# S5 parameters prepared on GpSimd beside the first layer's projections, kept in DRAM, and S5 inputs turned beside the retention heads

## What is computed

```python
    lam = lax.complex(lam_re.astype(f32), lam_im.astype(f32))
    delta = jnp.exp(log_step.astype(f32))[:, None]
    lam_bar = jnp.exp(lam * delta)
    b_bar = ((lam_bar - 1.0) / lam)[:, :, None] * b_mat
    bu = jnp.einsum('gpc,bsgc->bsgp', b_bar, uf.astype(jnp.complex64))
    a = jnp.broadcast_to(lam_bar, bu.shape)
    _, states = lax.associative_scan(combine, (a, bu), axis=1)
    y = jnp.einsum('gcp,bsgp->bsgc', c_mat, states).real + d_skip.astype(f32) * uf
```

## Time and profile before

| | us |
|---|---|
| median of 3 runs | 3587.89 (3587.1 to 3588.26) |
| profiled execution | 3577.61 |
| its span (first to last instruction) | 3575.8 |
| mean granted clock of TensorE | 0.923 of full speed |
| busy: PE, DVE, ACT, POOL | 3150.0, 2233.1, 1674.9, 79.6 |

### The profile page before, as it was taken

One profiled execution on the slowest core, in us unless ns is written; L12 is line 12 of the kernel. 1 busy time (PEld: TensorE's weight loads), 2 busy tenths in 40 slices (PEclk: granted clock), 3 DMA queues, 4 the chain that ended last, 5 costly groups with the idle time before them and its releaser, 6 DMA issues.

```text
span 3575.8 us, 37657 instructions
## 1 busy us (share of the span) xinstructions
PE 3150.0 (88%) x14074; PEld 2471.9 (69%) x14074; DVE 2233.1 (62%) x2597; ACT 1674.9 (47%) x1936; POOL 79.6 (2%) x88
## 2 busy tenths in 40 slices
PE   5896775999999999999959747999998987899998
PEld 2652464777777777777747635788887765688887
DVE  2314444999999999999965666443445545544445
ACT  2212132878787877878753112432335234432234
POOL 0000000000000000000030000000000000000000
PEclk8897775999999999999979876999999988999999
DMA  8142123999999999999952201223232210123320
GB/s 325 53 144 92 60 64 119 368 369 375 368 375 376 372 373 371 372 369 372 365 187 67 72 0 48 68 91 101 94 107 76 83 37 1 41 87 97 97 74 24
DMA packets 226419, 637.83 MB, mean 178 GB/s; under 512 B 21225, under 2 KB 39927, under 8 KB 226135
## 3 DMA queue, kind: packets, MB, share of 16 engines
q1 hardware_dynamic: 206880, 575.35, 44.8%
q0 software_dynamic: 10512, 37.80, 2.8%
q10 hardware_dynamic: 8838, 22.23, 1.7%
HBM read 605.94 MB, written 29.36 MB: 178 GB/s over the span
## 4 chain that ended last, share of the span: by engine, by line
PE 77%; DVE 14%; ACT 5%; issue 2%; DMA 1%; POOL 0%; DVEq 0%; ACTq 0%; POOLq 0%; SPq 0%
PE ps L267 74%; ACT arena L232 3%; PE ps L279 3%; DVE arena L187 2%; DVE arena L198 2%; ACT wunits L449 2%; DVE arena L206 2%; DVE arena L194 1%; DVE ring_r L457 1%; DVE arena L210 1%; DVE ring L187 1%; DVE arena L192 1%; DVE arena_r L457 1%; DVE arena_r L198 1%; ACT arena_r L232 1%
## 5 line engine op out<-in xcount | busy, mean ns | idle before, releaser
L457 DVE TENSOR_TENSOR ring_r<-ring,wunits 128x1024 fp32r<-128x1024 f32 x795 | 943.4, 1216 | 676.9 <-ACT wunits L449 659.6
L449 ACT ACTIVATE wunits<-ring 128x1024 fp32r<-128x1024 f32 x795 | 830.6, 1054 | 824.6 <-PE ps L267 796.4
L267 PE MATMUL ps<-arena_r,wunits 128*128 128x512 f32 x3552 | 1107.5, 394 | 60.9 <-DVE ring_r L457 34.1
L267 PE MATMUL ps<-wunits,arena_r 128*128 128x512 f32 x3520 | 989.5, 398 | 3.2 <-DVE arena_r L187 3.2
L267 PEld LDWEIGHTS ps<-arena_r,wunits 128*128 128x128 f32 x3552 | 670.2, 190 | 209.1 <-DVE ring_r L457 34.2
L267 PEld LDWEIGHTS ps<-wunits,arena_r 128*128 128x128 f32 x3520 | 658.2, 189 | 148.1 <-DVE arena_r L187 5.0
L267 PE MATMUL ps<-arena_r,ring_r 128*128 128x512 f32 x1776 | 693.6, 391 | 0.0
L267 PE MATMUL ps<-ring_r,arena_r 128*128 128x512 f32 x1280 | 409.8, 390 | 0.0
L267 PE MATMUL ps<-arena 128*128 128x128 f32 (+11 forms) x1378 | 276.2, 386 | 147.9 <-DVE arena L192 32.8
L267 PEld LDWEIGHTS ps<-arena_r,ring_r 128*128 128x128 f32 x1776 | 336.6, 190 | 70.5
L267 PEld LDWEIGHTS ps<-arena 128*128 128x128 f32 (+4 forms) x1378 | 204.8, 232 | 206.1 <-issue 42.9
(11 more groups left out here) (119 smaller groups left out, 1771.3 us busy)
## 6 DMA issues: line engine op xcount, KB each, us to landing
ring<-in_w_gu SPq DMA_DIRECT2D x382, 512.0 KB, 6.7
ring<-in_w_down SPq DMA_DIRECT2D x170, 512.0 KB, 5.4
arena<-in_w_gu SPq DMA_DIRECT2D x146, 512.0 KB, 6.8
arena<-in_w_down SPq DMA_DIRECT2D x94, 512.0 KB, 5.6
ring<-in_w_ada SPq DMA_DIRECT2D x48, 512.0 KB, 4.7
ring<-in_ffn_w_gate SPq DMA_DIRECT2D x44, 512.0 KB, 3.5
ring<-in_ffn_w_up SPq DMA_DIRECT2D x44, 512.0 KB, 3.6
ring<-in_ffn_w_down SPq DMA_DIRECT2D x40, 512.0 KB, 3.6
```

The source lines that it names most:

```text
L267: ins = self.e.matmul(o, l_, r_, start=start, stop=stop, skip_group_check=True)
L449: q.inc(q.e.activation(h, raw, ACT.Copy), (st.tag, "hi", i))
L457: q.inc(q.e.tensor_tensor(lo, raw, h.bitcast(F32), ALU.subtract), (st.tag, "lo", i))
```

## The change

`s5_prep_*` is split. The 32-column part (`s5_small_*`, the old code without the 128x512 operations) is the first `slow` work of `proj`, where four steps are added (9 of its 16 steps are used). The 128x512 operations go to GpSimd (`s5_pool`), in slots 9 to 17 of the ring, which the weights of the first layer do without until "s5 parked". The PE, DVE and ACT parts of it (`s5_large_*`) come after the eight `ada` generators in `slow`; `pool` gets four steps. The tables are written to DRAM: `s5_kk`, `s5_mg` in pieces by ACT's queue, `s5_gs`, `s5_ww` by POOL's. ACT loads the first two before the projections of `ret`, POOL the others in the S5 stage. The turning of `U3` is `slow` work of `heads`. The tables of the retention are loaded before the projections, no more behind the barrier "ret in". `AB` has a buffer for each direction, cleared once by DVE. The zeros are written later, for 14 blocks and not 15. POOL is no longer waited for at barriers.

```diff
...
     def barrier_of(q, key):
-        for table, s_ in ((at_pe, s_pe), (at_dve, s_dve), (at_act, s_act), (at_pool, s_pool)):
+        for table, s_ in ((at_pe, s_pe), (at_dve, s_dve), (at_act, s_act)):
...
+            elif w.before[0] == "pool":
+                s.wait_ge(*pool(w.before[1]))
...
-    W = main_stream("w", SLOTS)
+    PARK = SLOTS[9:]
+    W = main_stream("w", SLOTS[0:9])
...
     def widen():
-        if len(W.pieces) == N_FIRST + NRING:
-            W.slots = list(reversed(MORE)) + W.slots
+        if len(W.pieces) == N_FIRST + 9:
+            for x in PARK:
+                x[3] = ("pool", "s5 parked")
+            W.slots = PARK + MORE + W.slots
...
-    def zero_pool(g):
-        g.inc(g.e.memset(ZB, 0.0), "zeros")
-        g.own()
-        load(g, "zero", y_d[4096:NBLK * 128, :].rearrange("(b p) d -> p b d", p=128),
-             ZB.unsqueeze(1).to_broadcast([128, NBLK - 32, 1024]))
...
             p.note(("w", "used", u.i))
+            p.step()
...
             p.note(("pool", g))
+            p.step()
...
+    def power(g, dst, X, XI_, i, sign, key):
+        g.tt(ptmp, XI_, bc(sl(AI, i)), ALU.mult)
+        g.tt(dst, X, bc(sl(AR, i)), ALU.mult)
+        g.tt(dst, dst, ptmp, ALU.add if sign > 0 else ALU.subtract, key)
+    def s5_pool(g):
+        g.wait_ge(*loaded("s5b"))
+        g.ts(BI[0:64, :, :], BI[0:64, :, :], -1.0, None, ALU.mult, None)
+        g.wait_ge(*dve("s5 f"))
+        g.tt(ptmp, BI, bc(FI), ALU.mult)
+        g.tt(PA, B0, bc(FR), ALU.mult)
+        g.tt(PA, PA, ptmp, ALU.add, "s5 pa")
+        g.tt(ptmp, B0, bc(FI), ALU.mult)
+        g.tt(PI_, BI, bc(FR), ALU.mult)
+        g.tt(PI_, PI_, ptmp, ALU.subtract)
+        g.wait_ge(*act("s5 qi"))
+        for tau in range(1, 9):
+            power(g, GP[:, :, tau - 1, :], QA, QI, tau, -1, ("s5 q", tau))
+        g.own()
+        g.e.dma_start(gs_d, BUF).then_inc(s_gsd, 16)
+        g.wait_ge(s_gsd, 16)
+        g.wait_ge(*pe("s5 k", 7))
+        for s_ in range(8):
+            power(g, GP[:, :, s_, :], PA, PI_, 7 - s_, 1, "s5 pm")
+        g.fill(ptmp, 0.0)
+        g.own()
+        load(g, "zero", y_d[33 * 128:, :].rearrange("(p b) (h d) -> p (b h) d", p=128, d=512),
+             pw(6144, 512).unsqueeze(1).to_broadcast([128, 2 * (NBLK - 33), 512]))
+        WR_, WI_ = pw(0, 2048, 64), pw(2048, 2048, 64)
+        TT1, TT2 = pw(4096, 1024), pw(5120, 1024)
+        g.wait_ge(*pe("s5 mt", 28))
+        g.copy(WR_[:, :, 0:1], WC.unsqueeze(2))
+        g.copy(WI_[:, :, 0:1], WS.unsqueeze(2))
+        m_ = 1
+        while m_ < 64:
+            br_ = WR_[:, :, m_ - 1:m_].to_broadcast([128, 32, m_])
+            bi_ = WI_[:, :, m_ - 1:m_].to_broadcast([128, 32, m_])
+            x1 = TT1[:, 0:32 * m_].rearrange("p (g n) -> p g n", n=m_)
+            x2 = TT2[:, 0:32 * m_].rearrange("p (g n) -> p g n", n=m_)
+            g.tt(x1, WR_[:, :, 0:m_], br_, ALU.mult)
+            g.tt(x2, WI_[:, :, 0:m_], bi_, ALU.mult)
+            g.tt(WR_[:, :, m_:2 * m_], x1, x2, ALU.subtract)
+            g.tt(x1, WR_[:, :, 0:m_], bi_, ALU.mult)
+            g.tt(x2, WI_[:, :, 0:m_], br_, ALU.mult)
+            g.tt(WI_[:, :, m_:2 * m_], x1, x2, ALU.add)
+            m_ *= 2
+        g.own()
+        g.e.dma_start(ww_d, BUF).then_inc(s_wwd, 16)
+        g.wait_ge(s_wwd, 16)
+        for s_ in s_kst:
+            g.wait_ge(s_, 8 * 16)
+        g.wait_ge(*loaded("zero"))
...
+    def s5_large_pe(p):
+        p.wait_ge(*pool("s5 pa"))
+        for tau in range(8):
+            name = ("s5 k", tau)
+            b = p.bank(name)
+            if tau:
+                p.wait_ge(*pool("s5 q", tau))
+            p.claim(name)
+            for j in range(4):
+                q_ = GP[:, 8 * j:8 * j + 8, tau - 1, :] if tau else QA[:, 8 * j:8 * j + 8, :]
+                p.mm(PB[b][:, j * 128:(j + 1) * 128], PAf[:, j * 128:(j + 1) * 128], q_, j == 0, j == 3,
+                     name if j == 3 else None)
+            if tau % 2:
+                yield
+        for g0 in range(0, 32, 4):
+            name = ("s5 mt", g0)
+            b = p.bank(name)
+            p.wait_ge(*pool("s5 pm"))
+            p.claim(name)
+            for g in range(4):
+                p.tp(PB[b][:, g * 128:(g + 1) * 128], BUF[:, (g0 + g) * 128:(g0 + g + 1) * 128],
+                     name if g == 3 else None)
+            if g0 % 8:
+                yield
+    def s5_large_dve(v):
+        v.wait_ge(*loaded("s5b16"))
+        for tau in range(8):
+            x = KST[tau % 2].rearrange("p (j c) -> p j c", c=128)
+            if tau >= 2:
+                v.wait_ge(s_kst[tau % 2], 16 * (tau // 2))
+            else:
+                v.wait_ge(*pe("s5 c"))
+            v.wait_ge(*pe("s5 k", tau))
+            v.tt(x, bank_of(("s5 k", tau))[:, :].rearrange("p (j c) -> p j c", c=128),
+                 b16.unsqueeze(1).to_broadcast([128, 4, 128]), ALU.mult, ("s5 kk", tau))
+            v.free(("s5 k", tau))
+            if tau == 0:
+                for j in range(4):
+                    v.stt(x[:, j, :], ident, C("s5d", j), x[:, j, :], ALU.mult, ALU.add, ("s5 kk", 0))
+            if tau % 2:
+                yield
+        for g0 in range(0, 32, 8):
+            yield
+    def s5_large_act(q):
+        for tau in range(8):
+            q.wait_ge(*dve("s5 kk", tau))
+            q.e.dma_start(kk_d[:, tau * 512:(tau + 1) * 512], KST[tau % 2]).then_inc(s_kst[tau % 2], 16)
+            if tau % 2:
+                yield
+        for i, g0 in enumerate(range(0, 32, 4)):
+            name = ("s5 mt", g0)
+            q.wait_ge(s_kst[i % 2], 16 * (4 + i // 2))
+            q.wait_ge(*pe(*name))
+            q.copy(KST[i % 2], bank_of(name)[:, :], name)
+            q.free(name)
+            q.own()
+            q.e.dma_start(mg_d[:, g0 * 128:(g0 + 4) * 128], KST[i % 2]).then_inc(s_kst[i % 2], 16)
+            if i % 2:
+                yield
...
-    AB = [a(10496, 512), a(11008, 512)]
+    AB = [[a(23040, 512), a(23552, 512)], [a(10496, 512), a(11008, 512)]]
...
                     all_wait(v, "gla 0")
+                    for x in AB[0] + AB[1]:
+                        v.fill(x, 0.0)
...
-                    v.wait_ge(*pool("cleared", ci, hl))
...
-    def gla_pool(g):
-        for ht in range(2):
-            for d in range(2):
-                ci = 2 * ht + d
-                if ci == 0:
-                    all_wait(g, "gla 0")
-                for hl in range(2):
-                    g.wait_ge(*pe("scores", ci, hl))
-                    g.inc(g.e.memset(AB[hl], 0.0), ("cleared", ci, hl))
...
     def ret_pe(p):
-        p.slow.append(s5_prep_pe(p))
...
-    DT, KD, QD_, CD, B64 = a(6272, 1024), a(7296, 512), a(3200, 512), a(7936, 4), a(7808, 128)
+    DT, KD, QD_, CD, B64 = a(21504, 1024), a(22528, 512), a(23040, 512), a(23680, 4), a(23552, 128)
...
+    def turned_in_pe(p):
+        for j in range(4):
+            for x in range(2):
+                name = ("un", j, x)
+                b = p.bank(name)
+                p.claim(name)
+                for s_ in range(4):
+                    p.tp(PB[b][0:64, s_ * 128:(s_ + 1) * 128], U3[:, j, 4 * x + s_::8], name if s_ == 3 else None)
+            yield
+            name = ("ug", j)
+            b = p.bank(name)
+            p.wait_ge(*act("un", j, 1))
+            p.claim(name)
+            for g in range(8):
+                p.tp(PB[b][:, g * 64:(g + 1) * 64], ar[0:64, 6272 + g * 128:6272 + (g + 1) * 128],
+                     name if g == 7 else None)
+            yield
+    def turned_in_act(q):
+        for j in range(4):
+            for x in range(2):
+                name = ("un", j, x)
+                q.wait_ge(*pe(*name))
+                if j:
+                    q.wait_ge(*pe("ug", j - 1))
+                q.copy(UNj[:, :, 4 * x:4 * x + 4, :],
+                       bank_of(name)[0:64, :].rearrange("p (s g c) -> p g s c", s=4, c=16), name)
+                q.free(name)
+            yield
+            name = ("ug", j)
+            q.wait_ge(*pe(*name))
+            q.copy(UG[:, 8 * j:8 * j + 8, :], bank_of(name)[:, :].rearrange("p (g n) -> p g n", n=64), name)
+            q.free(name)
+            yield
+    def turned_in_dve(v):
...
     def heads_pe(p):
+        p.slow.append(turned_in_pe(p))
...
     def s5_in_pe(p):
-        p.inuse.extend(range(4))
-        for j in range(4):
-            p.bank(("y5", j), at=j)
...
-            uv = U3[:, j, :].rearrange("p (n t) -> p n t", t=8)
-            for tau in range(8):
-                p.mm(yv[:, :, tau:8], KK[:, tau * 4 + j, :], uv[:, :, 0:8 - tau], tau == 0, False, count=tau == 7)
...
-        p.wait_ge(*act("un", 7))
...
-        p.wait_ge(*act("ug", 24))
+        p.wait_ge(*loaded("s5mg"))
+        p.wait_ge(*act("ug", 3))
         for g0 in range(0, 32, 8):
             name = ("vv", g0)
             b = p.bank(name)
...
                 p.mm(PB[b][:, g * 64:(g + 1) * 64], MG[:, (g0 + g) * 128:(g0 + g + 1) * 128], UG[:, g0 + g, :],
```

(67 more changed lines are left out.)

466 lines of the change are left out of this document (191 added, 275 removed).

## The result

The changed kernel took 3564.86 us (median, 3562.05 to 3570.21) against 3588.07 us for the kernel before: a ratio of 0.9937, 95% interval 0.992 to 0.9955. It is 23 us faster, where 44.6 had been forecast; the time lies inside the stated range.

The account below looks back on a forecast made before the run. PE was taken to bound the kernel (77% of the chain), so gains lie where PE waits. Late −70.6 plus front +26.0 gave −44.6: 3533.0 profiled, 3543.3 us with the median's 10.28 offset; range 3518 to 3572.

Parts of the forecast that it names:

- its own sign: Front: the forecast is wrong if the projections and `pool` lengthen by more than 10 us.
- the 35 foretold: End of gla: PE idle ahead of the output projection for 35 us in place of 15.34.
- (a): Start of heads: with the table loaded earlier, PE's 14.0 us pause becomes 5.0, so −9.0.
- (b): Heads: table work goes from the end, repeated passes and first pass, against added `U3` turns: −34 us, bounds 30 and 38.
- Rival 3: Late stages give less, with PE at clock 0.50 through heads and S5: sum −24.6, time 3563; 15%.
- (c): S5 stage: 99.0 us becomes 72.7, PE's local part running beside DVE's rotation and scan: −26, bounds 20 and 33.
- (d): Front, small things: parameter loads +0.5, `proj` +2.7, `pool` and `gates` +7.2, fills +2.0, clears −5.8; sum +6.6 us.
- (e): End of gla: GpSimd's 24 operations for tables P, 1.35 us each, then turn and writes, delay the barrier: +19.4 us.
- (f): Front: tables Q, running phases, zeros, nine ring slots and the ring's late release put at no cost.
- Rival 2: Wait at gla's end nearly vanishes: 0.75 us for each GpSimd operation makes it 5.0, time 3529; 12%.
- Rival 1: Slower: GpSimd's P operations set gla's end, cancelling the gain at 3.2 us each; at 4.0 the time is 3607; 8%.
- Rival 4: Savings return as a wait: phases at three times their price, MoE waits 30 to 45 us; time 3583, no difference; 5%.

Follow-up runs that it names:

- turns_after: Changed kernel with the turns of the S5 inputs made at the end of heads, not beside its passes: 3574.4 us, 8 to 10 us slower than the changed kernel.
- p_twice: Changed kernel with GpSimd making the tables P twice over (48 operations in place of 24): 3593.56 us, 27 to 29 us slower than the changed kernel.

## Why the prediction held, and where it failed

The sign held, and so did the mechanism of the gain; the size is half of the forecast. That the time lies inside the range owes something to luck: the front cost 69.0 us where its bounds were 8 and 40, `heads` gave 41.3 where they were 30 and 38, and these two misses partly cancel. Two of the signs that the forecast named need a word. `proj` and `pool` lengthened by 20.9 us together, and by its own sign it is wrong there, above 10 (though its terms for the two already made 13.5). And the pause of 36.89 us looks like the 35 foretold, but by chance: the forecast meant all that PE stands still behind gla, which is 12.82 + 36.89 us. Point by point:

- **(a)** held: 4.95 us left of 14.00. Of what went, 5.9 were the load; the other 3.2 are put down to the parameter work.
- **(b)** `heads` gave 41.3 and not 34: the end went in full (25.4), the part ahead of the three repeated passes gave 12.9 for 8, and the passes 3.1, where the 8.7 of DVE and the 7 set against them leave 1.7. The turns of `U3` cost 3.2 us and not 7 + 7, by turns_after. So the term is mis-sized on the good side. But the last two passes did not become 2.9 us shorter each: they are 16.30 and 17.26 us for 17.53 and 17.31, and the turns are not the cause, as turns_after shows. DVE's work went and PE waited less for it (3.55 us for 5.86), but the granted clock, 0.80 and 0.78 in these passes before, was 0.82 and 0.50. Rival 3 had named that clock.
- **(c)** held step by step. The phases landed at 22.5 us of the stage (forecast 22 to 23), the scan ended at 33.9 (34.4), the local part at 36.5 (39), the three operations at 47.7 (50.5), the stage at 69.9 (72.7). The 3 us better are the local part, which ended 2.5 us earlier, and `zi` at the higher clock (3.62 us for 4.5).
- **(d)** failed in size: +29.1 for +6.6. The start: the parameter loads cost 4.0 to 7.5 us (6.9 between the two profiles) and not 0.5. `pool`: the three halves are there (24 products, 11.1 us), but PE also waits 3.13 for weights of `ada` and 3 us more for the gates' weights. The issues of SP, before and after, point to why:

```profile
169.22 106.78 SPq L436 DMA_DIRECT2D ring<-in_w_ada  x30
```
```profile
231.02 68.33 SPq L438 DMA_DIRECT2D ring<-in_w_ada  x25
```

  With nine slots the weights of `ada` are issued from 231.02 on, when `pool` begins at 231.82, and no longer 50 us ahead of it. The prediction's "nine slots serve in front" had this at nothing. No run gives the slots back, so the cause of these 6 us is read from rows and not shown by an experiment. `gates` was to lose a half and did not: one stands just behind the scan (319.43, 4.88 us, where a turn of 0.55 stood before), where PE resumes and the next stage waits. I had counted the halves and not looked at which place each falls on.
- **(e)** was the deciding term, and its parts failed unequally. P started where it was said (427 and the shift of 29 is 456). t was 1.23 us for 1.35, so 2.9 us better. The chain behind it took 26.5 and not 12.2 us, +14.3; from the barrier to the output projection went 15.9 and not 6.9, +9.0. 19.4 − 2.9 + 14.3 + 9.0 = 39.8, the 39.9 measured. The estimate from the Trainium skill (GPSIMD Engine Reference, § 3.1), 1.12 us, was as near to t as mine: 2.5 us too low for the path, mine 2.9 too high.
- **(f)** is the step that failed behind it: "the zeros are written while nothing else writes much" and the phases "at nothing". The duration of the phases was right (35.5 us for 35), the cover held (parked at 534, MoE at 667), but both shared something with the path: the zeros the DMA engines with the pieces, at a DMA share of 1.02, the phases SBUF with DVE. The experiments on them give 18.8 and 9.1 us.
- **Rivals.** None took over as written. Rival 2, a wait that nearly vanishes, needed t = 0.75. Rival 1 has the right place, and p_twice shows its price for each operation; its point of no gain lies near 2.2 us (23 us of gain over 24 operations, on top of 1.23) and not at 3.2, since the rest of the sum was smaller. Rival 3, a smaller gain late, did not come; its 3563 is the time measured, by another cause. Rival 4 did not come.

## What to carry over

Work sent to an idle engine is not free because it ends in time: ask of each of its DMAs and operations what runs at that moment on the path, and whether they share the DMA engines or SBUF with it. Where side work has a chain of its own (here product, table, turn, write), the first link decides: setting it ahead of other filler, with no operation less, gained 60 us, more than twice what the whole change had. Count filler by the place it falls on, not by its sum. And ask of a late release (here "s5 parked") what it lets start, and beside what.

## What the runs showed of the hardware

- GpSimd's two-input operation on 128x512 takes 1.20 to 1.23 us with DVE at little work and 1.34 beside the projections (40.09 us for 30); DVE's 0.69.
- It slows DVE in turn: 128x1024 with both inputs in SBUF went from 1.22 to 2.9 us beside operations on up to 128x1024, to 1.49 beside the short ones (means of one). In gla, the same 36 operations cost nothing that can be seen (149.4 us with them, 150.0 without).
- A 7 MB write from one queue makes 256 KB writes of another land in 6.8 in place of 2.0 us. Beside nine 512 KB loads from SP's queue, 512 KB writes of ACT's land in 4.2 to 4.4 us in place of 2.6.
- Thirteen small loads of GpSimd's queue, issued beside it, delay a 2 MB load from 8.0 (8.1 with the loads behind it) to 11.1 us, 9.6 to 12.4 over eleven profiles.
- PE's 26 products of a pass of `heads` took 6.60 to 6.83 us at a mean granted clock of 0.78 to 0.82, and 9.45 at 0.50.
